# The 16-key tail of attention's product with the values: an fp32 product of 128 rows, or one fp32r product with three stacked parts

## The reference, cut to what matters

```python
s = jnp.einsum("bhcqd,bhckd->bhcqk", qblk, k)      # c: two components of 64
p = jax.nn.softmax(s, axis=-1)
a = p[:, :, 0] - lam * p[:, :, 1]
return jnp.einsum("bhqk,bhkv->bhqv", a, v)         # v: 128 wide
```

## Time and profile before

| | us |
|---|---|
| median of 3 runs (1891.81 to 1892.63) | 1892.57 |
| profiled execution, its own time | 1891.99 |
| span of that execution | 1890.2 |
| TensorE busy | 1865.8 (99%) |
| VectorE busy | 1260.3 (67%) |
| ScalarE busy | 877.4 (46%) |
| GpSimd busy | 1161.7 (61%) |
| products with the values (L1261), first to last start | 980.6 to 1348.2 |

### The profile page before, as it was taken

The page is one execution under the profiler, slowest core; times in us unless marked ns, Lnnn a source line. Parts: engine busy times, 40 slices in busy tenths (PEclk is TensorE's granted clock), DMA queues, the critical chain, the costliest instruction groups (busy, mean ns, idle before and its releaser), DMA issues.

```text
span 1890.2 us, 31720 instructions
## 1 busy us (share of the span) xinstructions
PE 1865.8 (99%) x10933; PEld 1749.9 (93%) x10933; DVE 1260.3 (67%) x2156; ACT 877.4 (46%) x1847; POOL 1161.7 (61%) x1533
## 2 busy tenths in 40 slices
PE   7999999999999999999999999999999999999999
PEld 7888888899999999999988888888889999999998
DVE  7857575778767676657776666666487575756673
ACT  5434433446444444454534444444465454544453
POOL 4534535358787878687843333332458787887885
PEclk9999999999999999999999999999999999999999
DMA  5559999527879797784376656656133435353534
GB/s 175 195 183 265 237 277 227 166 82 181 227 193 282 194 271 198 249 239 138 98 164 127 124 118 124 124 114 117 53 94 111 139 107 149 97 156 101 153 114 130
DMA packets 379273, 307.03 MB, mean 162 GB/s; under 512 B 14291, under 2 KB 322294, under 8 KB 378886
## 3 DMA queue, kind: packets, MB, share of 16 engines
q1 hardware_dynamic: 348592, 235.32, 41.2%
q0 software_dynamic: 28416, 69.21, 20.3%
q10 hardware_dynamic: 2134, 0.82, 0.2%
HBM read 299.70 MB, written 144.02 MB: 235 GB/s over the span
## 4 chain that ended last, share of the span: by engine, by line
PE 90%; DVE 6%; ACT 2%; issue 1%; POOL 0%; DMA 0%; ACTq 0%; DVEq 0%; POOLq 0%
PE ps L943 50%; PE ps L850 25%; PE ps L1100 3%; PE ps L1261 3%; PE ps L1229 2%; PE ps L1251 1%; PE ps L1079 1%; PE ps L1163 1%; ACT wt L2496 1%; PE ps L1109 1%; DVE sx L1499 0%; PE ps L1354 0%; PE ps L1193 0%; DVE gt L1606 0%; PE ps L1061 0%
## 5 line engine op out<-in xcount | busy, mean ns | idle before, releaser
L943 PE MATMUL ps<-sx,wh 128*128 128x400 f32 (+1 forms) x2044 | 530.5, 340 | 0.9 <-POOL wl L774 0.5
L774 POOL TENSOR_TENSOR wl<-raw,wh 128x256 fp32r<-128x256 f32 (+1 forms) x432 | 355.1, 853 | 98.5 <-ACT wh L2176 97.0
L740 POOL CAST wh<-raw 128x256 fp32r<-128x256 f32 x248 | 102.8, 456 | 478.5 <-PE ps L850 432.7
L943 PEld LDWEIGHTS ps<-sx,wh 128*128 128x128 f32 x2044 | 373.4, 188 | 2.8 <-ACT gt_first L2191 0.9
L943 PE MATMUL ps<-sx,wl 128*128 128x400 f32 (+1 forms) x1022 | 347.6, 340 | 0.0
L774 POOL TENSOR_TENSOR wl<-raws,wh 128x256 fp32r<-128x256 f32 x328 | 282.3, 905 | 84.8 <-ACT wh L2176 84.3
L1660 DVE TENSOR_TENSOR h<-h,ps 128x400 f32<-128x400 f32 (+1 forms) x280 | 154.4, 559 | 131.6 <-PE ps L943 131.5
L943 PE MATMUL ps<-fx,wh 128*128 128x400 f32 (+1 forms) x904 | 235.4, 341 | 0.3 <-issue 0.2
L850 PE MATMUL ps<-xh,wh 128*128 128x512 f32 (+1 forms) x752 | 211.8, 358 | 0.0
L850 PE MATMUL ps<-xl,wh 128*128 128x512 f32 (+1 forms) x752 | 207.3, 349 | 0.0
L744 POOL TENSOR_TENSOR wl<-raw,wh 128x256 fp32r<-128x256 f32 x248 | 199.0, 830 | 5.1
(11 more groups left out here) (317 smaller groups left out, 3622.8 us busy)
## 6 DMA issues: line engine op xcount, KB each, us to landing
in_sums<-in_ffn_w_in_dram SPq DMA_DIRECT2D x16, 1536.0 KB, 9.4
raw<-in_sums SPq DMA_DIRECT2D x96, 256.0 KB, 3.1
in_sums<-in_ffn_w_in_dram SPq DMA_DIRECT2D x16, 1280.0 KB, 7.6
raw<-in_ffn_w_in_dram SPq DMA_DIRECT2D x80, 256.0 KB, 3.0
raws<-in_sums SPq DMA_DIRECT2D x80, 256.0 KB, 3.0
raw<-out_sums SPq DMA_DIRECT2D x120, 128.0 KB, 2.7
raws<-in_ffn_w_in_dram SPq DMA_DIRECT2D x52, 256.0 KB, 3.4
raw<-in_m_w_in_dram SPq DMA_DIRECT2D x24, 512.0 KB, 4.1
```

What stands on the lines that cost most here:

```text
L740: ins = pool.tensor_copy(wh[:, slot, c], raw[:, slot, c])
L774: ins = pool.tensor_tensor(slot_of(n, 1)[:, c], raw_of(n)[:, c], slot_of(n, 0)[:, c].bitcast(F32), ALU.subtract)
L943: mm = pe.matmul(product_bank(layer, s, j), slot_of(n, low_w)[:, k * P:(k + 1) * P], x, start=(j in OPENS and k + q == 0), stop=(k == tile ...
```

## The change

The 16-key tile gets operands of its own type and layout. `at_r` and `va_r` are fp32r views of the same memory. Of the 128 rows that the array multiplies, the 16-key tile used rows 0 to 15. Now rows 0 to 15 hold the high part, rows 32 to 47 the second part and rows 64 to 79 the third, so that one fp32r product adds up all three partial products: weights high by values high, weights high by values low, weights low by values high. In `at_r` the three are high, high, low; in `va_r` high, low, high. The rows between stay zero.

ScalarE writes the high part of the weights first, then the full tiles. VectorE makes the low part (PSUM minus the high part) and copies the high part to rows 32 to 47, in `turned_low`, once for each query block; for the values it makes the low part in `values_low`, once for each head. ScalarE writes the values' high part twice. TensorE's `attend` waits for VectorE's two steps too, ahead of its first product.

```diff
+        va_r, at_r = place(SPLIT_X + 4 * 4 * LENS[0], ("va_r", [P, 2, NT, P], F32R), ("at_r", [P, 2, 5, P], F32R))
...
-            for x in (at[:, :, :, :], va[:, :, :, :]):
-                pool.memset(x, 0.0).then_inc(attn_zeroed, 1)
+            for x in (at_r[:, :, 4, :], va_r[:, :, 4:8:3, :]):
+                pool.memset(x.bitcast(F32), 0.0).then_inc(attn_zeroed, 1)
...
                 pe.wait_ge(at_ready, hd * NQ + (i + 1))
+                pe.wait_ge(at_low, hd * NQ + (i + 1))
                 if i == 0:
-                    pe.wait_ge(va_ready, hd * 3 + 3)
-                js = OF_SEQ[Q_SEQ[i]]
-                for q, j in enumerate(js):
-                    mm = pe.matmul(acc_o, at[:, i % 2, q, :], va[:, odd, j, :],
-                                   start=(q == 0), stop=(j == js[-1]), skip_group_check=True)
-                mm.then_inc(o_done, 1)
+                    pe.wait_ge(va_ready, hd * 4 + 4)
+                    pe.wait_ge(va_low, hd + 1)
+                *full, short = OF_SEQ[Q_SEQ[i]]
+                for q, j in enumerate(full):
+                    pe.matmul(acc_o, at[:, i % 2, q, :], va[:, odd, j, :], start=(q == 0), stop=False,
+                              skip_group_check=True)
+                pe.matmul(acc_o, at_r[:, i % 2, 4, :], va_r[:, odd, short, :], start=False, stop=True,
+                          skip_group_check=True).then_inc(o_done, 1)
...
+            def values_low(hd, odd):
+                ve.wait_ge(va_ready, hd * 4 + 4)
+                ve.tensor_tensor(va_r[HIGH_AGAIN, odd, 4:8:3, :],
+                                 turn_bank.rearrange("p (i c) -> p i c", i=4)[0:META, 2:4, :],
+                                 va_r[0:META, odd, 4:8:3, :].bitcast(F32), ALU.subtract).then_inc(va_low, 1)
+
+            def turned_low(hd, i):
+                ve.wait_ge(at_short, hd * NQ + (i + 1))
+                high = at_r[0:META, i % 2, 4, :].bitcast(F32)
+                ve.tensor_tensor(at_r[LOW_ROWS, i % 2, 4, :], ps[0:META, 5, 0:P], high, ALU.subtract)
+                ve.tensor_copy(at_r[HIGH_AGAIN, i % 2, 4, :], high).then_inc(at_low, 1)
...
+                if not first:
+                    turned_low(hd - 1, NQ - 1)
                 combine(hd, 0)
...
                 combine(hd, 1)
+                values_low(hd, odd)
                 if last:
                     add_tile(OUT1, EARLY[0], 3)
                 else:
                     evacuate(n, 3, kx)
+                turned_low(hd, 0)
                 maxima(hd, odd, 2)
...
+                turned_low(hd, 1)
                 combine(hd, 2)
...
                 combine(hd, 3)
+                turned_low(hd, 2)
...
+                turned_low(hd, 3)
                 combine(hd, 4)
...
                 if not first:
                     scale_output(hd - 1, even)
 
+                turned_low(hd, 4)
                 if last:
                     add_tile(OUT1 + 2, EARLY[2], 3)
...
             head(D_HEADS - 1, 1, None, last=True)
+            turned_low(D_HEADS - 1, NQ - 1)
             output(D_HEADS - 1, 1, NQ - 1)
...
-                    sc.activation(va[0:META, odd, 4:8:3, :], src[0:META, 2:4, :], ACT.Copy).then_inc(va_ready, 1)
+                    for rows in (slice(0, META), LOW_ROWS):
+                        sc.activation(va_r[rows, odd, 4:8:3, :], src[0:META, 2:4, :], ACT.Copy).then_inc(va_ready, 1)
...
-                sc.activation(at[:, i % 2, 0:full, :], ps[:, 4, 0:full * P].rearrange("p (q c) -> p q c", q=full), ACT.Copy)
-                sc.activation(at[0:META, i % 2, full, :], ps[0:META, 5, 0:P], ACT.Copy).then_inc(at_ready, 1)
+                sc.activation(at_r[0:META, i % 2, 4, :], ps[0:META, 5, 0:P], ACT.Copy).then_inc(at_short, 1)
+                sc.activation(at[:, i % 2, 0:full, :], ps[:, 4, 0:full * P].rearrange("p (q c) -> p q c", q=full),
+                              ACT.Copy).then_inc(at_ready, 1)
```

More of the change, by code:

```diff
@@ L55 @@
 OF_SEQ = ([0, 1, 2, 3, 4], [5, 6, 7])
+SHORT = (4, 7)
+HIGH_AGAIN, LOW_ROWS = slice(32, 32 + META), slice(64, 64 + META)
 NT = len(TILES)
@@ L527, in trunk @@
         sums_fourth = [sem("sums_fourth0"), sem("sums_fourth1")]
+        va_low, at_short, at_low = sem("va_low"), sem("at_short"), sem("at_low")
         maskb_in, attn_zeroed = sem("maskb_in"), sem("attn_zeroed")
@@ L1200, in turn_values @@
                 else:
-                    pe.wait_ge(va_ready, hd * 3 + 1)
+                    pe.wait_ge(va_ready, hd * 4 + 1)
                 for q, i in enumerate(((0, 1, 2, 3), (5, 6, 4, 7))[part]):
```

## The result

| | us |
|---|---|
| before, median of 4 runs in the comparison (1891.81 to 1892.63) | 1892.35 |
| changed kernel, median of 4 runs (1907.45 to 1909.98) | 1908.69 |
| ratio, with its 95% interval | 1.0087 (1.0073 to 1.0102) |
| profiled execution of the changed kernel: own time, span | 1909.98, 1908.2 |
| forecast, range | 1897.2, 1892.0 to 1901.0 |

A forecast was written before the change was run, and what follows sets the result against it. TensorE, busy 99% of the span, was taken as the bound. Savings of 3.0 us against waits of 7.7 for VectorE's added pair gave net +4.7 and a forecast of 1897.2 us, range 1892.0 to 1901.0.

The forecast's parts named there:

- The new product costs 0.112 and saves 0.112: Short key tile on TensorE: one fp32r record replaces two fp32 records; 27 savings reach the end, 3.0 us.
- attend 0's saving: First query block's attend: its 0.112 was counted as reaching the end in seven middle heads and the last.
- The pair's two durations: VectorE's added 16x128 subtract and cast for each query block: 0.29 and 0.21 us.
- 0.47 from the pair's start to its end and 0.39 until the operation behind may start: VectorE's subtract and cast together, assuming the last 0.08 overlaps the next operation; low end 0.30, high 0.9 to 1.0.
- the key roots: Pair for attend 3 delays VectorE's chain to the key roots' turning: 0.39 in seven heads, 2.73 us.
- A VectorE result reaches TensorE some 0.06 later: Delay from VectorE's end to TensorE's start, used at attend 0 to place its start at 1125.13.
- GpSimd's casts may hold the cast a little: Attend 0: VectorE's cast among GpSimd's casts; wait taken as 0.35, ends 0.18 and 0.9, 2.45 in seven heads.
- the rival of the collision: VectorE's cast waits for a whole GpSimd operation at attends 0 and 5: 14 × 0.36, 1902.2; chance 0.11.
- Attend 5, "TensorE at 1112.56 in place of 1112.54": Attend run in the next head, pair behind the evacuation: 0.05 each with GpSimd's casts, 0.35 in seven.
- The last head, attend 4: Pair ahead of the next output tile's add delays that add and TensorE's block: 1.0 us.
- the net of +13.2: Sum with the pair at its high end: waits 16.2 us, needing every cast to be caught by GpSimd.

The follow-up runs named there:

- i_low_first: Against the kernel where ScalarE makes the second high copy: low part moved to rows 0 to 15, high parts to rows 32 and 64; 1897.03, ratio 1.0027.
- m_no_hold: i_low_first with the high part in its own tile in rows 0 to 15, copied by ScalarE to rows 32 and 64; 1894.61, ratio 1.0015.
- c_quadrant0: Changed kernel with VectorE's subtract and cast both writing to scratch tiles in partitions 0 to 15; 1897.46, ratio 1.0027.
- j_all: m_no_hold with attend 0's subtract ahead of the evacuation, value waits first, last head's subtracts for attends 4 and 5 moved; 1891.78, ratio 1.0000.
- q_roots_first: j_all with combine(4) moved behind the first normalise_k on VectorE; 1891.65, ratio 0.9997.

## Why the prediction was wrong, step by step

- **"The new product costs 0.112 and saves 0.112": right.** The differences fall by 0.11 to 0.15 at each attend, and the product alone gave 2.6 against 3.0. That attend 0's saving reaches the end in the middle heads was wrong (0.10 of it is lost in front of attend 1), and a little larger saving of the others made up for most of it.
- **The pair's two durations: right, where GpSimd is idle.** 0.28 and 0.22 against 0.29 and 0.21, over 48 pairs (the pace worked out from the two subtracts is 1.05 ns for a column and not 1.03, which changes nothing):

```profile
L2045 DVE TENSOR_TENSOR at_r<-ps,at_r x48: 281/282/283, 981.2 to 1364.9; 16x128 fp32r<-16x128 f32 x48
...
L2046 DVE CAST at_r<-at_r x48: 216/217/658, 981.5 to 1365.2; 16x128 fp32r<-16x128 f32 x48
```

- **"0.47 from the pair's start to its end and 0.39 until the operation behind may start": wrong, and the step that failed.** I took the overlap of 0.08 from operations that all start in partition 0 and gave it to two that start in 32 and 64. At the key roots 0.58 lie between its neighbours (1154.22 to 1154.80), which overlapped by 0.08 without it: 0.66 instead of 0.39 (the turning is late by 0.64 to 0.67). The kernel with both outputs in partition 0 has 0.30 there. The key roots of a seventh head, made in head 6, were counted too and aren't late: there TensorE comes some 1.0 behind the copy.
- **"A VectorE result reaches TensorE some 0.06 later": too small.** It is 0.15 with one wait and 0.33 at attend 0, where two more stand behind it. My row was of TensorE's turning, whose wait for VectorE is the last thing before its product. The diff that put two waits behind the new one was in front of me, and I gave them no price. Why one wait makes 0.15, where the turning of the key roots still starts 0.06 behind its copy (1156.64 and 1156.70), was not tested.
- **"GpSimd's casts may hold the cast a little": right in size, and the rival had the mechanism.** The cast takes 0.35 at attend 0 and at attend 5, and up to 0.66. It does wait until the running GpSimd operation is over, as the rival of the collision says, in 16 of 48 casts. The rival's 0.36 for each was too much, because the cast comes 0.13 behind the start of a GpSimd cast and would have taken 0.22 anyway: 0.13 is left. That I had it small was luck of the moment at which it starts; where it met a subtract of GpSimd the same wait cost 0.44.
- **Attend 5, "TensorE at 1112.56 in place of 1112.54": wrong by the same two errors.** The pair ends at 0.68 behind the evacuation and not at 0.39 (0.13 of it is the wait for GpSimd), and TensorE starts 0.15 later: late by 0.39 in six heads and by 0.26 in the seventh, where the cast takes 0.22.
- **Not in the forecast: the second turning of values.** It looked covered, since nothing waited there. VectorE's steps behind the pair slip, one of them into the wait for GpSimd, and ScalarE's copy of the values with them: 2.1, which is gone in the kernel without the cast, but for the last head.
- **The last head, attend 4: "1.0" was right in mechanism** (the block waits 1.82 in place of 0.47), but the pair was mis-sized there too, 1.35 instead of 1.0, because the cast took 0.40 and the gaps came on top; and in the profiled execution the clock's drop added 1.6.

So direction and mechanism were right, and the size was off by a factor of more than three, because nearly every term carried the same pair. The range was too narrow for that: its upper end, 1901.0, lies below the net of +13.2 that the prediction itself works out for the pair's high end, because this "needs every cast to be caught by GpSimd"; but one error in the shared term moved all of them together, and the measured 16.3 lies above that net too.

## What to carry to other kernels

When small operations are added to an engine that works close in front of TensorE, look at the partitions where their operands and results start, not only at their durations: 0.5 us of work cost 0.7 here, and with the same work in partitions 0 to 15 two thirds of the loss were gone, directly and by what it set free behind it. Look also at what GpSimd runs at the moment when a VectorE copy within SBUF starts: the copy ended only 0.08 behind that operation, so a shift of 0.13 in its start took its duration from 0.35 to 0.21. Put the wait that decides last in the list, and keep an engine's late-coming result out of the first product where only the last needs it. When one estimated size enters the sum many times, widen the range by that size times its count.

## What the hardware showed that I had not expected

- A VectorE operation that starts in another group of 32 partitions than its neighbour, by its output or by an SBUF input, starts up to 0.03 after it instead of 0.07 to 0.08 before it. The input alone does it: in i_low_first the subtract starts 0.03 behind the end of the operation ahead of it (1149.03 against 1149.00), in m_no_hold 0.08 before it (1147.83 against 1147.91).
- VectorE's small cast from SBUF to SBUF, when it starts during an operation of GpSimd, ends 0.07 to 0.08 behind that operation's end if its own 0.22 would be over sooner: 16 of 48 in the changed kernel (0.35 to 0.66), and 0.40 once in c_quadrant0. The subtract with an input in PSUM never did.
- On TensorE each satisfied semaphore wait with a value computed in the loop, standing behind the one that decides, costs 0.09 (0.33 with two, 0.15 with none).
- TensorE's clock fell to half for 3.3 us behind an idle time of 1.82 that followed full work, in some executions and not in others.
- In j_all, m_no_hold and q_roots_first, where ScalarE has two copies more for each query block, the second turning of the output is late by 0.28 in head 2 and by 0.09 in heads 4 and 6, and not in heads 1, 3 and 5, which are the same code in the loop's first half. ScalarE's copy in front of it starts 0.27 later in head 2 and 0.08 later in the other two, with nothing to wait for. The cause is open.
